# A transformer block kernel: the norm's power moved from before the first projection to behind it

## The chip, the cores and the metric

The kernel runs on one core of one Trainium2 chip. The metric is the device time of one execution in microseconds (us). A core has TensorE (PE, matrix products, reads SBUF and writes PSUM), VectorE (DVE), ScalarE (ACT), GpSimd (POOL) and the DMA queues that SyncE (SP) and ScalarE issue. Each engine works through a program of its own in order and waits on semaphores that others raise.

## The reference, cut to what matters

The computation is two transformer blocks on 512 tokens of width 1024. The first has a mixer (sparse attention with compressed keys, and a gated MLP) and a feed-forward layer; the second has differential attention, pooling, 32 experts and a gated embedding. The change touches only the first norm and the projection w_in (1024 to 2328 columns) behind it:

```
def rms_norm(x, g):
    y = xf * lax.rsqrt(jnp.mean(xf * xf, axis=-1, keepdims=True) + RMS_EPS)
    return (y * g.astype(jnp.float32)).astype(x.dtype)
...
    proj = jnp.einsum("bsd,de->bse", h, w_in)      # h = rms_norm(x, norm_mix_pre)
    q, k_c, v_c, k_s, v_s, k_w, v_w, gate_logits, u, v = jnp.split(proj, points, axis=-1)
...
    z_u = jax.nn.gelu(u)
    z_v = layer_norm(jax.nn.gelu(v), gmlp_ln_g, gmlp_ln_b)
```

The factor rsqrt(mean + eps) belongs to a token, the gain g to a column of x. So the factor may be put on the tokens ahead of the projection or on its outputs.

## The kernel before, in words

Everything runs as one program without loops at run time. Each weight matrix is streamed by SP as chunks of up to 128x2048 floats into three slots of RING (`sp_load`, L218). A chunk is split into a high part WH (ScalarE, `act_split`, L230) and a low remainder WL (VectorE, `dve_split`, L245), and each product is made of three matmuls (high by high, high by low, low by high: `pe_mm3`, L255 to L257). Chunk c+3 is loaded into the slot of chunk c once its low part is made.

Start (`*_start`): SP loads the tokens X as four tiles of 128 (L567). ScalarE issues the small loads (constants CST with the identity, nine rows of gains and tables, L570 to L579), then squares the four tiles with a running sum (L584). VectorE turns each sum into a mean (L655), POOL raises it to the power -0.5 (L598, into R4), and VectorE multiplies the tile by it (`rows`, L659, into XR0). TensorE transposes the 84 rows of gains (L603, from VectorE's copy L668 they are in GT) and then the four normed tiles, 8 transposes each, to the 8 banks PS0 to PS7 (L609). Bank j then holds rows 128j of the transposed tokens for all 512 tokens. ScalarE writes each bank times the gain as high part (`act_put`, L327), VectorE the low part (`dve_put`, L334).

Projection (`*_win`): the columns come in groups of two chunks (the upper and the lower half of the 1024 rows). Chunks 0 and 1 make 3 outputs of 128 columns by 512 tokens (compressed keys and values k_c and v_c, and k_s) in banks 0 to 2; chunks 2 and 3 make the 4 outputs of q in banks 0 to 3; chunks 4 and 5 make k_w in bank 3 and 4 outputs of 128 tokens by 280 columns in banks 4 to 7; chunks 6 to 9 are the first weights of the compression, used as they come (L749); chunks 10 to 13 make u and v. An output of a chunk with 512 free columns is 4 rows of weights by 3 matmuls, 12 in all. Behind single outputs `behind` lets TensorE make pieces of the position bias from a table: one "far" product (L620), four "near" groups of 64 small matmuls (L627) and four "cmp" groups of 31 (L634), all in bank 7, each copied by VectorE (L639, L643, L650) before the next may write the bank. The near groups stand behind outputs of chunks 1 and 2, the cmp groups behind outputs 2 and 3 of chunk 2 and outputs 0 and 1 of chunk 3.

The outputs of chunks 1, 3 and 5 leave PSUM by ScalarE (L780, L786, L799, L801). ScalarE issues DMAs of k_c and v_c to the other half of the partitions (L784). In `dve_win` VectorE makes, in this order: the far copy, the low part of chunk 3, the near and cmp copies, `blocks(0)` (4 additions of position rows to k_c, L861, waiting for those DMAs), the low part of chunk 4, `blocks(1)`, the low part of chunk 5. TensorE waits for the low part of a chunk before its first matmul.

## Time and profile before

| | |
|---|---|
| median of 3 runs | 2118.5 us (2116.66 to 2118.97) |
| the profiled execution's own time | 2118.25 us |
| its span | 2116.4 us |
| PE busy | 2060.8 us (97%) |
| DVE busy | 1537.0 us (73%) |
| ACT busy | 1383.2 us (65%) |
| chain that ended last | PE 91%, DVE 5%, issue 1%, ACT 1%, DMA 1% |

All times in the rows are microseconds from the span's start unless marked ns. Matmuls overlap, so one's duration is longer than its distance to the next.

### The profile page before, as it was taken

Reading aid. Unit: us, or ns where it says so; the run is one execution under the profiler, and the core shown is the slowest. Engines: PE = TensorE matmul, PEld = TensorE weight load, DVE = VectorE, ACT = ScalarE, POOL = GpSimd, SP = SyncE. Lnnn points to the kernel's source line nnn. Section 1 sums busy time; section 2 is a strip of 40 time slices with the busy share of each in tenths; the row PEclk is TensorE's granted clock in tenths of the full one; section 3 lists DMA queues with packets and bytes.
Section 4 is the critical chain, followed back from the end, with each engine's and each line's share of the span. In section 5 each row is a group of like instructions: output and inputs, shape, how many; then the busy total and the mean of one; then the engine's idle time right before and its main releaser. Section 6 shows DMA issues by size and latency. Waiting matters only on the chain.

```text
span 2116.4 us, 31589 instructions
## 1 busy us (share of the span) xinstructions
PE 2060.8 (97%) x10497; PEld 1707.9 (81%) x10497; DVE 1537.0 (73%) x1825; ACT 1383.2 (65%) x1870; POOL 194.8 (9%) x232
## 2 busy tenths in 40 slices
PE   7998899999999999899999999999999999999998
PEld 6887788888887887778888888888888888888877
DVE  4357743332325677789899999989898989898984
ACT  3247643222323447478888888888888888888863
POOL 0000000000000000111111111111111111111110
PEclk9999999999999999999999999999999999999999
DMA  6321013222323311489999999999999999999971
GB/s 199 135 71 61 21 55 124 87 94 80 120 100 103 117 72 41 171 307 373 369 372 367 370 369 371 369 366 375 366 379 363 370 372 372 361 371 371 376 264 40
DMA packets 86560, 511.27 MB, mean 242 GB/s; under 512 B 17285, under 2 KB 18905, under 8 KB 29146
## 3 DMA queue, kind: packets, MB, share of 16 engines
q1 hardware_dynamic: 71312, 487.61, 61.2%
q0 software_dynamic: 9680, 17.33, 3.2%
q10 hardware_dynamic: 5498, 5.39, 0.9%
q8 instruction: 45, 0.74, 0.1%
q14 instruction: 25, 0.20, 0.0%
HBM read 503.44 MB, written 23.07 MB: 249 GB/s over the span
## 4 chain that ended last, share of the span: by engine, by line
PE 91%; DVE 5%; issue 1%; ACT 1%; DMA 1%; ACTq 0%; POOL 0%; DVEq 0%; SPq 0%; POOLq 0%
PE PS L2595 17%; PE PS L2597 17%; PE PS L2596 17%; PE PS L255 10%; PE PS L257 10%; PE PS L256 10%; PE PS L2478 1%; PE PS L2592 1%; PE PS L2605 1%; PE PS L1153 1%; PE PS L1865 1%; DVE AR L1124 1%; PE PS L1082 0%; PE PS L1800 0%; PE PS L1793 0%
## 5 line engine op out<-in xcount | busy, mean ns | idle before, releaser
L2472 DVE TENSOR_TENSOR WL<-RING,WH 128x2048 fp32r<-128x2048 f32 x385 | 873.5, 2288 | 95.6 <-ACT WH L2452 92.5
L2452 ACT ACTIVATE WH<-RING 128x1024 fp32r<-128x1024 f32 x770 | 806.4, 1059 | 163.1 <-PE PS L2597 157.5
L2595 PE MATMUL PS<-WH,RA 128*128 128x512 f32 x1540 | 628.5, 408 | 0.0
L2597 PE MATMUL PS<-WH,RA 128*128 128x512 f32 x1540 | 600.7, 390 | 0.0
L2596 PE MATMUL PS<-WL,RA 128*128 128x512 f32 x1540 | 600.4, 390 | 0.0
L2597 PEld LDWEIGHTS PS<-WH,RA 128*128 128x128 f32 x1540 | 289.5, 188 | 61.7
L2596 PEld LDWEIGHTS PS<-WL,RA 128*128 128x128 f32 x1540 | 289.9, 188 | 58.1
L2595 PEld LDWEIGHTS PS<-WH,RA 128*128 128x128 f32 x1540 | 290.8, 189 | 55.3
L255 PE MATMUL PS<-WH,RA 128*128 128x512 f32 (+1 forms) x560 | 219.4, 392 | 3.4 <-DVE WL L245 2.2
L257 PE MATMUL PS<-WH,RA 128*128 128x512 f32 (+1 forms) x560 | 216.1, 386 | 0.0
L256 PE MATMUL PS<-WL,RA 128*128 128x512 f32 (+1 forms) x560 | 215.8, 385 | 0.0
L250 DVE SCALAR_TENSOR_TENSOR WL<-RING,GT,WH 128x512 fp32r<-128x512 f32 x120 | 82.2, 747 | 167.7 <-ACT WH L235 167.6
L235 ACT ACTIVATE WH<-RING,GT 128x512 fp32r<-128x512 f32 x120 | 76.8, 713 | 175.2 <-PE PS L257 175.2
L255 PE MATMUL PS<-RA,WH 128*128 128x512 f32 (+1 forms) x448 | 168.7, 377 | 3.3 <-DVE RA L458 1.6
L256 PE MATMUL PS<-RA,WH 128*128 128x512 f32 (+1 forms) x448 | 167.6, 374 | 0.0
L257 PE MATMUL PS<-RA,WL 128*128 128x512 f32 (+1 forms) x448 | 167.6, 374 | 0.0
L245 DVE TENSOR_TENSOR WL<-RING,WH 128x2048 fp32r<-128x2048 f32 (+3 forms) x29 | 62.3, 2150 | 92.0 <-ACT WH L230 91.8
L255 PEld LDWEIGHTS PS<-WH,RA 128*128 128x128 f32 x560 | 105.7, 189 | 24.1 <-DVE WL L245 2.3
L257 PEld LDWEIGHTS PS<-WH,RA 128*128 128x128 f32 x560 | 105.7, 189 | 21.2
L256 PEld LDWEIGHTS PS<-WL,RA 128*128 128x128 f32 x560 | 105.8, 189 | 20.2 <-issue 0.2
L230 ACT ACTIVATE WH<-RING 128x2048 fp32r<-128x2048 f32 (+3 forms) x29 | 52.1, 1801 | 105.5 <-PE PS L257 95.9
L2757 POOL DMA_INDIRECT acc_scr<-AR,SMALL x32 | 69.9, 2185 | 464.8 <-issue 464.8
(395 smaller groups left out, 2265.9 us busy)
## 6 DMA issues: line engine op xcount, KB each, us to landing
RING<-w_experts SPq DMA_DIRECT2D x390, 1024.0 KB, 7.3
RING<-w_front SPq DMA_DIRECT2D x58, 1024.0 KB, 4.9
X<-x SPq DMA_DIRECT2D x4, 512.0 KB, 5.6
...
```

The costliest lines, as they stand in the source:

```text
L235: x = e.activation(WH[:, ch.buf, v], RING[:, ch.slot, v], ACT.Copy, scale=GT[:, g:g + 1])
L245: x = e.tensor_tensor(WL[:, ch.buf, 0:n], RING[:, ch.slot, 0:n], WH[:, ch.buf, 0:n].bitcast(F32), ALU.subtract)
L250: x = e.scalar_tensor_tensor(WL[:, ch.buf, v], RING[:, ch.slot, v], GT[:, g:g + 1], WH[:, ch.buf, v].bitcast(F32), ALU.mult, ALU.subtract)
L255: e.matmul(out, a[0], b[0], start=start, stop=False)
L256: e.matmul(out, a[0], b[1], start=False, stop=False)
L257: return e.matmul(out, a[1], b[0], start=False, stop=stop)
L2452: e.activation(WH[:, m % 3, v], RING[:, m % 6, v], ACT.Copy).then_inc(s("m_hi"), 1)
L2472: e.tensor_tensor(WL[:, m % 3, :], RING[:, m % 6, :], WH[:, m % 3, :].bitcast(F32), ALU.subtract).then_inc(s("m_lo"), 1)
L2595: e.matmul(PS[bank][:, :], lhs[0][:, kr + k, :], WH[:, m % 3, c], start=(sel is None and kr == 0 and k == 0), stop=False)
L2596: e.matmul(PS[bank][:, :], lhs[0][:, kr + k, :], WL[:, m % 3, c], start=False, stop=False)
L2597: x = e.matmul(PS[bank][:, :], lhs[1][:, kr + k, :], WH[:, m % 3, c], start=False, stop=(stop and k == 3))
L2757: e.indirect_dma_start(acc_d, bass.IndirectOffsetOnAxis(TCOL, 0), YY, None, bounds_check=511, oob_is_err=False, compute_op=ALU.add).then_i ...
```

## The change: what it does

The transposes read the tokens X as they are loaded. Only the 8 rows of the first gain are waited for ahead of them; the 84 rows are transposed behind output 0 of chunk 0 (`pe_gains`), which waits until all 8 low parts of the tokens are made, because it writes bank 7. The squares, means and powers come behind that work on their engines. Chunk 0 is split in two halves, between the second and the third of the 8 tiles of tokens.

VectorE multiplies the identity by each token tile's power (RDG), TensorE multiplies an all-ones block by it (`pe_norm_row`, behind output 1 of chunk 1), and VectorE copies the result to RROW: every partition then holds the 512 powers. The eight outputs that have tokens as columns leave PSUM by VectorE, times RROW (`dve_project_out`), and no longer by ScalarE. The outputs that have tokens as rows take the power as a per-partition factor of the instruction that evicted them already (the copies of VSG, the activations of u and v).

The bias groups move: the far product to output 0 of chunk 2, the near groups to outputs 1 to 3 of chunk 2 and output 0 of chunk 3, the cmp groups 0 and 1 to outputs 1 and 2 of chunk 3, and both of the cmp groups 2 and 3 behind its output 3 (group 3 in bank 6).

```diff
-            e.wait_ge(s("w_lo"), ch.split + 1)
+            e.wait_ge(*((s("w_lo"), ch.split + 1) if c else (s("w_lo0"), 1)))
...
+                    if c == 0 and o == 0 and k == 2:
+                        e.wait_ge(s("w_lo"), 1)
...
-            for n, g in enumerate(("norm_mix_pre", "norm_ffn_pre", "attn_norm_2", "ffn_norm_2", "ple_gate_norm_2")):
-                e.dma_start(AR[n * 8:n * 8 + 8, 0:128], A[g].rearrange("o (a b) -> (o a) b", b=128)).then_inc(s("d_gr"), 16)
+            e.dma_start(AR[0:8, 0:128], A["norm_mix_pre"].rearrange("o (a b) -> (o a) b", b=128)).then_inc(s("d_g0"), 16)
+            for n, g in enumerate(("norm_ffn_pre", "attn_norm_2", "ffn_norm_2", "ple_gate_norm_2")):
+                e.dma_start(AR[n * 8 + 8:n * 8 + 16, 0:128], A[g].rearrange("o (a b) -> (o a) b", b=128)).then_inc(s("d_gr"), 16)
...
+            e.wait_ge(s("v_win"), AT["v_gt"] + 1)
+            for j in range(8):
+                if j == 2:
+                    e.wait_ge(s(f"w_ld{CH[0].slot}"), CH[0].loaded)
+                    for half in range(2):
+                        v = slice(CH[0].w * 2 * half, CH[0].w * (2 * half + 2))
+                        e.activation(WH[:, CH[0].buf, v], RING[:, CH[0].slot, v], ACT.Copy).then_inc(s(("w_hi0", "w_hi")[half]), 1)
+                act_put(e, XT["mix"] + j, j, PS[j][:, :], GT[:, j:j + 1])
+            act_split(e, 1)
             for i in range(4):
                 e.wait_ge(s(f"d_x{i}"), 16)
                 if i >= 2:
                     e.wait_ge(s("a_ss"), i - 1)
                 e.activation(WK[:, (i % 2) * 1024:(i % 2) * 1024 + 1024], X[:, i, :], ACT.Square,
                              accum_out=SSN[:, i:i + 1]).then_inc(s("a_ss"), 1)
-            act_split(e, 0)
-            e.wait_ge(s("v_win"), AT["v_gt"] + 1)
-            for j in range(8):
-                act_put(e, XT["mix"] + j, j, PS[j][:, :], GT[:, j:j + 1])
-            act_split(e, 1)
             act_split(e, 2)
+        RDG = cols(o_v, 4, 128)
+        RROW = VC.rearrange("p g h d -> p (g h d)")
+        def dve_project_out(e, n, dst):
+            bank = (0, 1, 2, 0, 1, 2, 3, 3)[n]
+            e.wait_ge(s("p_pr"), CH[(1, 1, 1, 3, 3, 3, 3, 5)[n]].first_out + (1, 2, 3, 1, 2, 3, 4, 1)[n])
+            if dst is None:
+                e.scalar_tensor_tensor(QT[:, bank, :], PS[bank][:, :], 0.125, RROW, ALU.mult, ALU.mult).then_inc(s("v_ev"), 1)
+            else:
+                e.tensor_tensor(dst, PS[bank][:, :], RROW, ALU.mult).then_inc(s("v_ev"), 1)
...
-            e.wait_ge(s("d_gr"), 16 * 9)
-            e.transpose(PS[7][:, 0:84], GR, IDT[0:84, 0:84]).then_inc(s("p_tab"), 1)
+            e.wait_ge(s("d_g0"), 16)
+            e.transpose(PS[7][:, 0:8], GR[0:8, :], IDT[0:8, 0:8]).then_inc(s("p_tab"), 1)
             for i in range(4):
-                e.wait_ge(s("v_xr"), i + 1)
+                e.wait_ge(s(f"d_x{i}"), 16)
                 for j in range(8):
                     if i == 0 and j == 7:
                         e.wait_ge(s("v_win"), AT["v_gt"] + 1)
-                    x = e.transpose(PS[j][:, i * 128:(i + 1) * 128], XR0[i][:, j * 128:(j + 1) * 128], IDT)
+                    x = e.transpose(PS[j][:, i * 128:(i + 1) * 128], X[:, i, j * 128:(j + 1) * 128], IDT)
                     if i == 3:
                         x.then_inc(s("p_xt"), 1)
+        def pe_gains(e):
+            e.wait_ge(s("d_gr"), 16 * 8)
+            e.wait_ge(s("v_xt"), XT["mix"] + 8)
+            e.transpose(PS[7][:, 0:84], GR, IDT[0:84, 0:84]).then_inc(s("p_tab"), 1)
+        def pe_norm_row(e):
+            for i in range(4):
+                e.wait_ge(s("v_dg"), i + 1)
+                x = e.matmul(PS[6][:, 128 * i:128 * i + 128], CST[:, 377:378].broadcast_to([128, 128]), RDG[:, i, :], start=True, stop=True)
+            x.then_inc(s("p_nr"), 1)
...
-            e.wait_ge(s("v_win"), AT["v_bf"] + 5 + i)
+            e.wait_ge(s("v_win"), AT["v_bf"] + 5 + min(i, 2))
             for c in range(31):
                 off = 511 + 128 * i - 16 * c - 31
-                x = e.matmul(PS[7][:, c * 8:c * 8 + 8], OH2[0:97, off:off + 128], T3[0:97, 24:32], start=True, stop=True)
+                x = e.matmul(PS[7 - i // 3][:, c * 8:c * 8 + 8], OH2[0:97, off:off + 128], T3[0:97, 24:32], start=True, stop=True)
...
-            def rows(i):
-                e.wait_ge(s("g_r4"), POW["mix"] + i)
-                e.tensor_scalar(XR0[i], X[:, i, :], R4[:, i:i + 1], None, ALU.mult).then_inc(s("v_xr"), 1)
-
-            mean(0)
-            mean(1)
-            rows(0)
-            mean(2)
-            rows(1)
-            mean(3)
             e.wait_ge(s("p_tab"), AT["p_gt"] + 1)
-            e.tensor_copy(GT[:, 0:84], PS[7][:, 0:84]).then_inc(s("v_win"), 1)
-            rows(2)
-            rows(3)
-            dve_split(e, 0)
+            e.tensor_copy(GT[:, 0:8], PS[7][:, 0:8]).then_inc(s("v_win"), 1)
             for j in range(8):
+                if j == 2:
+                    for half in range(2):
+                        v = slice(CH[0].w * 2 * half, CH[0].w * (2 * half + 2))
+                        e.wait_ge(s(("w_hi0", "w_hi")[half]), 1)
+                        e.tensor_tensor(WL[:, CH[0].buf, v], RING[:, CH[0].slot, v], WH[:, CH[0].buf, v].bitcast(F32), ALU.subtract
+                                        ).then_inc(s(("w_lo0", "w_lo")[half]), 1)
                 dve_put(e, XT["mix"] + j, j, PS[j][:, :], GT[:, j:j + 1])
             dve_split(e, 1)
+            for i in range(4):
+                mean(i)
+            for i in range(4):
+                e.wait_ge(s("g_r4"), POW["mix"] + i)
+                e.tensor_scalar(RDG[:, i, :], IDT, R4[:, i:i + 1], None, ALU.mult).then_inc(s("v_dg"), 1)
             dve_split(e, 2)
+            e.wait_ge(s("p_nr"), 1)
+            e.tensor_copy(RROW, PS[6][:, :]).then_inc(v_c.sem, v_c.up())
+            e.wait_ge(v_c.sem, v_c.n)
+            dve_project_out(e, 0, KCT[0])
+            e.wait_ge(s("p_tab"), AT["p_gt"] + 2)
+            e.tensor_copy(GT[:, 0:84], PS[7][:, 0:84]).then_inc(s("v_win"), 1)
...
+            def gains(e, o):
+                if o == 0:
+                    pe_gains(e)
+            pe_project(e, 0, outs, XP, 0, 8, {n: [("v_xt", XT["mix"] + n + 1)] for n in range(3)}, xt, behind=gains)
             def biases(e, o):
+                if o == 1:
+                    pe_norm_row(e)
+            def more_biases(e, o):
                 if o == 0:
                     pe_bias_far(e)
                 else:
                     pe_bias_near(e, o - 1)
-            def more_biases(e, o):
-                if o < 2:
-                    pe_bias_near(e, o + 2)
-                else:
-                    pe_bias_cmp(e, o - 2)
-
             pe_project(e, 1, outs, XP, 4, 8, {}, xt, behind=biases)
             outs = [(m, PS[m][:, :], "w", m * 128, 128) for m in range(4)]
-            free = {0: [("a_win", AT["a_kct"] + 1)], 1: [("a_win", AT["a_kct"] + 2)], 2: [("a_win", AT["a_kts"] + 1)]}
+            free = {0: [("v_ev", AT["v_kct"] + 1)], 1: [("v_ev", AT["v_kct"] + 2)], 2: [("v_ev", AT["v_kts"] + 1)]}
             def last_biases(e, o):
-                if o < 2:
-                    pe_bias_cmp(e, 2 + o)
+                if o == 0:
+                    pe_bias_near(e, 3)
+                else:
+                    pe_bias_cmp(e, o - 1)
+                if o == 3:
+                    pe_bias_cmp(e, 3)
             pe_project(e, 2, outs, XP, 0, 8, free, {}, behind=more_biases)
             pe_project(e, 3, outs, XP, 4, 8, {}, {}, behind=last_biases)
             outs = [(3, PS[3][:, :], "w", 0, 128)] + [(4 + i, PS[4 + i][:, 0:280], i, 128, 280) for i in range(4)]
-            free = {3: [("a_win", AT["a_q"] + 4)], 7: [("v_win", AT["v_bc"] + 4)]}
+            free = {3: [("v_ev", AT["v_q"] + 4)], 6: [("v_win", AT["v_bc"] + 4)], 7: [("v_win", AT["v_bc"] + 3)]}
...
-                e.activation(KCT[n], PS[n][:, :], ACT.Copy).then_inc(s("a_win"), 1)
-            e.activation(KT4[:, 0, :], PS[2][:, :], ACT.Copy).then_inc(s("a_win"), 1)
-                e.activation(QT[:, m, :], PS[m][:, :], ACT.Copy, scale=0.125).then_inc(s("a_win"), 1)
-            e.activation(KT4[:, 2, :], PS[3][:, :], ACT.Copy).then_inc(s("a_win"), 1)
...
+                e.activation(U[:, i, :], PS[4 + i][:, :], ACT.Gelu_apprx_tanh, scale=R4[:, i:i + 1]).then_inc(s("a_win"), 1)
+                e.activation(V[:, i, :], PS[4 + i][:, :], ACT.Gelu_apprx_tanh, scale=R4[:, i:i + 1], accum_out=LNS[:, i:i + 1]).then_inc(s("a_win"), 1)
...
+            dve_project_out(e, 1, KCT[1])
+            dve_project_out(e, 2, KT4[:, 0, :])
             dve_bias_far(e)
             dve_split(e, 3)
             for kb in range(4):
                 dve_bias_near(e, kb)
-            for i in range(4):
-                dve_bias_cmp(e, i)
+            dve_project_out(e, 3, None)
+            dve_bias_cmp(e, 0)
+            dve_project_out(e, 4, None)
+            dve_bias_cmp(e, 1)
+            dve_project_out(e, 5, None)
+            dve_bias_cmp(e, 2)
+            dve_project_out(e, 6, None)
+            dve_bias_cmp(e, 3)
             blocks(0)
             dve_split(e, 4)
             blocks(1)
             dve_split(e, 5)
+            dve_project_out(e, 7, KT4[:, 2, :])
             for i in range(4):
                 e.wait_ge(s("p_pr"), CH[5].first_out + 2 + i)
-                e.tensor_copy(VSG[:, i, :], PS[4 + i][:, 0:280]).then_inc(s("v_win"), 1)
+                e.tensor_scalar(VSG[:, i, :], PS[4 + i][:, 0:280], R4[:, i:i + 1], None, ALU.mult).then_inc(s("v_win"), 1)
             for n in range(2):
                 e.memset(HID[n][:, :, :, 31:32], 0.0).then_inc(v_c.sem, v_c.up())
+            e.wait_ge(s("v_ev"), AT["v_kw"] + 1)
```

## Rows read from the trace of the kernel before

**Rows 1.** The page: busy time and share by engine, and the chain that ended last.
```profile
PE 2060.8 (97%) x10497; PEld 1707.9 (81%) x10497; DVE 1537.0 (73%) x1825; ACT 1383.2 (65%) x1870; POOL 194.8 (9%) x232
...
PE 91%; DVE 5%; issue 1%; ACT 1%; DMA 1%; ACTq 0%; POOL 0%; DVEq 0%; SPq 0%; POOLq 0%
```

**Rows 2.** The timeline of PE, 10 to 19: start, busy, line, count, [idle before].
```profile
10.14 0.37 PE L603 MATMUL PS<-CST,AR 84*128 84x84 f32 x1 [10.14 <-DMA AR<-gmlp_b_s]
11.15 6.22 PE L609 MATMUL PS<-CST,AR 128*128 128x128 f32 x32 [0.63 <-DVE AR L659]
18.31 0.47 PE L255 MATMUL PS<-RA,WH 128*128 128x512 f32 x1 [0.95 <-DVE RA L334]
```

**Rows 3.** Line L609 in two stretches, 14.2 to 14.7 and 16.6 to 17.0 (ns).
```profile
L609 PE MATMUL PS<-CST,AR x5: 421/421/421, 13.8 to 14.7; 128*128 128x128 f32 x5
...
L609 PE MATMUL PS<-CST,AR x6: 272/272/273, 16.4 to 17.0; 128*128 128x128 f32 x6
```

**Rows 4.** The timeline of DMA issues at the start, on ScalarE's and SP's queues.
```profile
1.17 0.57 ACTq L572 DMA_DIRECT2D AR<-norm_mix_pre  x1
...
4.71 0.40 ACTq L576 DMA_DIRECT2D AR<-gmlp_b_s  x1
```

**Rows 5.** Issue to landing: CST (L570), the tokens (L567), chunk 0 (L218, issued 2.99).
```profile
DMA to landing us min/median/max: 4.3/4.3/4.3
...
DMA to landing us min/median/max: 4.2/5.6/7.2
...
DMA to landing us min/median/max: 8.1/8.1/8.1
```

**Rows 6.** The timeline of ScalarE at the start.
```profile
8.05 1.06 ACT L584 ACTIVATE AR<-X 128x1024 f32<-128x1024 f32 x1
...
12.23 1.47 ACT L230 ACTIVATE WH<-RING 128x1536 fp32r<-128x1536 f32 x1
16.70 4.74 ACT L327 ACTIVATE RA<-PS,GT 128x512 fp32r<-128x512 f32 x8 [3.00 <-PE PS L609]
```

**Rows 7.** The timeline of VectorE at the start.
```profile
14.06 1.75 DVE L245 TENSOR_TENSOR WL<-RING,WH 128x1536 fp32r<-128x1536 f32 x1
17.42 5.36 DVE L334 SCALAR_TENSOR_TENSOR RA<-PS,GT,RA 128x512 fp32r<-128x512 f32 x8 [1.60 <-ACT RA L327]
22.84 4.09 DVE L245 TENSOR_TENSOR WL<-RING,WH 128x1536 fp32r<-128x1536 f32 x2
```

**Rows 8.** The timeline of PE, 60 to 70: the end of chunk 3, the start of chunk 4.
```profile
60.80 0.93 PE L634 MATMUL PS<-AR 97*128 97x8 bf16 x31
61.59 0.48 PE L255 MATMUL PS<-RA,WH 128*128 128x512 f32 x1
...
66.68 0.39 PE L256 MATMUL PS<-RA,WH 128*128 128x512 f32 x1
66.91 0.39 PE L257 MATMUL PS<-RA,WL 128*128 128x512 f32 x1
68.08 0.47 PE L255 MATMUL PS<-RA,WH 128*128 128x512 f32 x1 [0.78 <-ACT AR L799]
```

**Rows 9.** The timeline of VectorE and of ScalarE's queue around the cmp copies.
```profile
30.16 2.88 ACTq L784 DMA_DIRECT2D AR<-AR  x4
...
58.16 0.41 DVE L650 COPY AR<-PS 128x248 f32<-128x248 f32 x1 [3.20 <-PE PS L634]
...
62.11 3.90 DVE L861 TENSOR_TENSOR AR<-AR,GT 64x496 f32<-64x496 f32 x4
66.04 1.86 DVE L245 TENSOR_TENSOR WL<-RING,WH 128x1632 fp32r<-128x1632 f32 x1
```

**Rows 10.** The timeline of PE at the gap ahead of chunk 10.
```profile
102.64 0.80 PE L255 MATMUL PS<-WH,RA 128*128 128x512 f32 x1 [2.18 <-DVE WL L245]
```

**Rows 11.** Busy time in stretches: PE, PEld, DVE, ACT, POOL, granted clock, DMA share, GB/s.
```profile
107.00:108.00 1.00, 1.00 (x4) 0.74 (x3) 0.00 (x0) 0.98 (x2) 0.00 (x0) 0.50 0.83 172
108.00:109.00 1.00, 1.00 (x10) 1.00 (x8) 0.22 (x1) 0.89 (x1) 0.00 (x0) 0.80 0.78 279
```

More of the change, by code:

```diff
@@ L184, in program @@
         for parts in (
-                (("p_gt", 1), ("p_bf", 5), ("p_bc", 4)),
+                (("p_gt", 2), ("p_bf", 5), ("p_bc", 4)),
                 (("p_kc", 1), ("p_vc", 1), ("p_gm", 8)),
-                (("a_kct", 2), ("a_kts", 1), ("a_q", 4), ("a_kw", 1), ("a_hid", 2), ("a_sg", 1), ("a_u", 4), ("a_v", 4), ("a_lnv", 4)),
+                (("a_hid", 2), ("a_sg", 1), ("a_u", 4), ("a_v", 4), ("a_lnv", 4)),
+                (("v_kct", 2), ("v_kts", 1), ("v_q", 4), ("v_kw", 1)),
                 (("a_lam", 1), ("a_rope", 2), ("a_sr", 1), ("a_gk", 1)),
@@ L196, in program @@
                 (("v_lam", 2), ("v_ang", 1), ("v_sr", 1)),
-                (("v_gt", 1), ("v_t3", 1), ("v_bf", 5), ("v_bc", 4), ("v_blk", 8), ("v_vw", 4), ("v_hidr", 1), ("v_kc", 1), ("v_vc", 1), ("v_lnm", 1), ("v_wst", 2), ("v_zv", 1), ("v_gm", 8)),
+                (("v_gt", 2), ("v_t3", 1), ("v_bf", 5), ("v_bc", 4), ("v_blk", 8), ("v_vw", 4), ("v_hidr", 1), ("v_kc", 1), ("v_vc", 1), ("v_lnm", 1), ("v_wst", 2), ("v_zv", 1), ("v_gm", 8)),
         ):
@@ L554, in program @@
         KORD = [(x, p) for x in (0, 2, 1, 3) for p in range(2)]
-        XR0 = [ar(o_qt + 1024 * i, 1024) for i in range(4)]
         RS = ATS[:, 80:144]
@@ L649, in dve_bias_cmp @@
             e.wait_ge(s("p_tab"), AT["p_bc"] + i + 1)
-            e.tensor_copy(BC[:, i, :, 0:31], PS[7][:, 0:248].rearrange("p (c h) -> p h c", h=8)).then_inc(s("v_win"), 1)
+            e.tensor_copy(BC[:, i, :, 0:31], PS[7 - i // 3][:, 0:248].rearrange("p (c h) -> p h c", h=8)).then_inc(s("v_win"), 1)
         def dve_start(e):
@@ L710, in pe_win @@
             outs = [(n, PS[n][:, :], "w", n * 128, 128) for n in range(3)]
-            pe_project(e, 0, outs, XP, 0, 8, {n: [("v_xt", XT["mix"] + n + 1)] for n in range(3)}, xt)
+            def gains(e, o):
+                if o == 0:
+                    pe_gains(e)
+            pe_project(e, 0, outs, XP, 0, 8, {n: [("v_xt", XT["mix"] + n + 1)] for n in range(3)}, xt, behind=gains)
             def biases(e, o):
+                if o == 1:
+                    pe_norm_row(e)
+            def more_biases(e, o):
                 if o == 0:
@@ L745, in pe_win @@
                         if c % 2 == 0:
-                            e.wait_ge(*((s("a_win"), AT["a_q"] + 1 + 2 * n + m), (s("a_win"), AT["a_kw"] + 1))[n * m])
+                            e.wait_ge(*((s("v_ev"), AT["v_q"] + 1 + 2 * n + m), (s("v_ev"), AT["v_kw"] + 1))[n * m])
                         for k in range(8):
@@ L778, in act_win @@
             for n in range(2):
-                e.wait_ge(s("p_pr"), CH[1].first_out + n + 1)
-                e.activation(KCT[n], PS[n][:, :], ACT.Copy).then_inc(s("a_win"), 1)
-                e.wait_ge(s("a_win"), AT["a_kct"] + n + 1)
+                e.wait_ge(s("v_ev"), AT["v_kct"] + n + 1)
                 for g in range(2):
@@ L784, in act_win @@
                         e.dma_start(KK[n][64 * par:64 * par + 64, g, :], KCT[n][64 * g:64 * g + 64, :]).then_inc(s(f"d_kk{n}"), 16)
-            e.wait_ge(s("p_pr"), CH[1].first_out + 3)
-            e.activation(KT4[:, 0, :], PS[2][:, :], ACT.Copy).then_inc(s("a_win"), 1)
-            e.wait_ge(s("a_win"), AT["a_kts"] + 1)
+            e.wait_ge(s("v_ev"), AT["v_kts"] + 1)
             for half in range(2):
@@ L796, in act_win @@
             act_split(e, 5)
-            for m in range(4):
-                e.wait_ge(s("p_pr"), CH[3].first_out + m + 1)
-                e.activation(QT[:, m, :], PS[m][:, :], ACT.Copy, scale=0.125).then_inc(s("a_win"), 1)
-            e.wait_ge(s("p_pr"), CH[5].first_out + 1)
-            e.activation(KT4[:, 2, :], PS[3][:, :], ACT.Copy).then_inc(s("a_win"), 1)
-            e.wait_ge(s("a_win"), AT["a_kw"] + 1)
+            e.wait_ge(s("v_ev"), AT["v_kw"] + 1)
             for half in range(2):
@@ L873, in dve_win @@
             dve_split(e, 5)
+            dve_project_out(e, 7, KT4[:, 2, :])
             for i in range(4):
                 e.wait_ge(s("p_pr"), CH[5].first_out + 2 + i)
-                e.tensor_copy(VSG[:, i, :], PS[4 + i][:, 0:280]).then_inc(s("v_win"), 1)
+                e.tensor_scalar(VSG[:, i, :], PS[4 + i][:, 0:280], R4[:, i:i + 1], None, ALU.mult).then_inc(s("v_win"), 1)
             for n in range(2):
                 e.memset(HID[n][:, :, :, 31:32], 0.0).then_inc(v_c.sem, v_c.up())
+            e.wait_ge(s("v_ev"), AT["v_kw"] + 1)
             e.memset(VC, 0.0).then_inc(v_c.sem, v_c.up())
@@ L936, in pe_cmp_logits @@
                 e.wait_ge(s("v_win"), AT["v_kc"] + 1)
-                e.wait_ge(s("a_win"), AT["a_q"] + 4)
+                e.wait_ge(s("v_ev"), AT["v_q"] + 4)
             for par in range(2):
```

2 lines of the change are left out of this document (removed).

## The prediction

> **What bounds the kernel now.** I read the page first: TensorE is busy for 97% of the span and makes 91% of the chain that ended last [rows 1]. So a microsecond by which TensorE's work starts later or earlier near the beginning moves the end by about as much, as long as nothing behind it has slack to give back. The change touches the first 110 us only, so I then read, in this order, the timeline of each engine over the first 70 us and the chain of waits there, the DMA landings, and the granted clock by stretches. The reader is to see three places. First, the transposes begin at 11.15, the first projection matmul at 18.31, and TensorE runs from there without a gap worth the name until chunk 4 [rows 2, 8]. Second, at chunk 4 TensorE stands 0.78 us for ScalarE's eviction of q, and the low part of chunk 4 comes from VectorE at just the same time (66.04 + 1.86 = 67.9, against a start at 68.08) [rows 8, 9]. Third, a gap of 2.18 us at 102.6 is followed by 5.7 us in which the granted clock is 0.50 of full [rows 10, 11].
>
> **The start.** The transposes no longer wait for squares, powers and the normed copy; they wait for the constants (issued 0.72, landed 4.3 later: 5.0), the first token tile (0.71 + 4.2 = 4.9) and the first gain row. That row's landing is in no row; it is issued at 1.17 [rows 4, 5]. Between the constants' 4.3 us and the 5.4 us of the last gain row (issued 4.71, waited for until 10.14 [rows 2, 4]) it lands at 5.5 to 6.6; I take 5.6, nearer its neighbour in the queue. The last token tile lands at about 2.1 + 7.2 = 9.3 [rows 5]. One transpose takes the engine about 0.22 us (five start between 13.8 and 14.7) and later 0.11 (six between 16.4 and 17.0) [rows 3]: the column of the granted clock reads 1.00 before its first recorded change, but the durations of 421 and then 272 ns say that the first 5 us of TensorE's work went at the lower level, 1.2 GHz. ScalarE can write its first tile after the 25th transpose: 5.6 + 0.3 for the gain row + 25 x 0.216 = 11.3, somewhat less if the clock rises on the way. I take 10.9 (bounds 10.3 and 12.2). Before it was 16.70 [rows 6], so 5.8 us are won here.
>
> **What is given back at once.** The split of chunk 0, formerly done during the transposes (12.23 to 15.8 [rows 6, 7]), now stands between tile 2 and tile 3. Chunk 0 has landed (2.99 + 8.1 = 11.1 [rows 5]). The halves cost VectorE 1.75 / 2 = 0.9 each, ScalarE 0.75 each. VectorE is the slower of the two with 5.36 / 8 = 0.67 a tile [rows 7]: its first low tile starts 0.72 after ScalarE's first, the first half's low part is ready at 10.9 + 0.72 + 1.34 + 0.9 = 13.9, and the eighth tile at 10.9 + 0.72 + 5.4 + 1.8 = 18.8. TensorE starts at 14.0, runs rows 0 and 1, gets tile 3 at 15.6 and ends output 0 at 15.6 + 6 x 0.227 = 17.0 (0.227 is the distance of two matmuls at the full clock [rows 8]). There the moved transpose of the 84 gain rows waits for the eighth low tile, because it writes bank 7: 1.8 us of idle TensorE, with outputs 1 and 2 queued behind it. With 0.37 for the transpose [rows 2] and 24 x 0.227, chunk 0 ends at 24.6. Before it ended at 18.31 + 36 x 0.227 = 26.5. Of 5.8 us, 1.9 are left.
>
> **Squares, means, powers, identity times power, RROW.** ScalarE's four squares (1.06 each [rows 6]) now follow the split of chunk 1 and end near 23; TensorE asks for the result behind output 1 of chunk 1, at about 30, so POOL's powers and the four small products on VectorE have some 7 us of cover and I cost them at nothing. `pe_norm_row` is new on TensorE: 4 matmuls of the transposes' size, 0.11 to 0.22 each [rows 3], and the change of operand around them: 0.7 us (bounds 0.4 and 1.2). The copy to RROW and the first eviction on VectorE (2 x 0.7, as the puts of 128x512 from PSUM [rows 7]) are ready 1.4 us after it; TensorE has output 2 (2.7 us) meanwhile. The second and third evictions stand behind the table's small conversions, still ahead of chunk 2's second output. The eight evictions cost VectorE the same 0.6 to 0.75 each that they cost ScalarE, and there is idle VectorE time between the near copies. The factors in VSG, u and v ride in instructions that exist already: nothing (bounds 0 and 0.1 us each). The x, constant and RING loads keep their order and their queues.
>
> **Chunk 4, where the loss is.** Before, the last cmp copy was over at about 62.1, and `blocks(0)` (3.90) and the low part of chunk 4 (1.86) were hidden behind outputs 2 and 3 of chunk 3 [rows 9]. Now cmp groups 2 and 3 are issued by TensorE only behind output 3, and VectorE's program has the copies of both, and the eviction of output 3, ahead of `blocks(0)`. Call t the end of output 3, before at 67.14. After, t = 67.14 - 1.9 (won) + 0.7 (norm row) - 2 x 0.79 (two cmp groups that now come behind t; 0.79 is 61.59 - 60.80 [rows 8]) = 64.4. From t on: cmp group 2 on TensorE 0.95, its copy 0.4, the eviction 0.75, the copy of group 3 0.4 [rows 9], `blocks(0)` 3.9, the low part 1.9. Chunk 4 starts at t + 8.3 = 72.7, against 68.08 before: 4.6 us later, with TensorE idle for about 6.6 us. Chunk 5's low part follows 5.8 us later and has chunk 4's 8.9 us of matmuls as cover. Everything behind (the gap at 102.6 as well, which hangs on chunk 7's end, a load and a split) is released by TensorE's own progress, so it moves with it.
>
> **The clock.** After the 2.18 us gap the granted clock stood at 0.50, that is 1.2 GHz, from about 102 to 108.4 [rows 10, 11]; TensorE worked 5.7 us in it and did half of that: 2.85 us lost. A gap three times as long should cost it again: I add 2.8 (bounds 0, if the clock holds, and 2.9). In the start there are two more gaps, 2.5 us between transposes and first matmul and 1.8 us behind output 0; before it was 0.95 [rows 2]. Whether the clock is low in chunk 0's last two outputs I can't read off; I add 1.0 (bounds 0 and 2.9).
> The Trainium skill speaks against the change here: its page "TensorE: Matmul & The Clock Gate", section "HAM oscillation — how this bites in real kernels", says that an idle wait between bursts of matmuls puts TensorE back to half rate, and that the burst behind it starts cold each time. By that rule the 2.8 us are due, without it the sum is 2123.7; the trace agrees, with its 0.50 behind a gap of 2.18 us.
>
> **The sum.** 4.6 + 2.8 + 1.0 = +8.4 us on the profiled execution's own 2118.25 (span 2116.4 and 1.85 around it), which lies 0.25 below the median of the three: about 2126.6 us.
>
> **The rivals.**
> *The clock holds over the gap.* Chunk 4 starts 4.6 later and little else: 2118.25 + 4.6 + (0 to 1.0) = 2123 to 2124. For it: a gap of 0.95 us left no trace in the clock. Against: 2.18 us did. Chance 0.14.
> *Low clock at both ends.* The start's gaps cost their full 2.9, and a shifted later gap one more such stretch: 2128.5 to 2131. Chance 0.12.
> *VectorE gets past the late copies, so the change is faster.* Place: `blocks(0)` and the low part of chunk 4 (5.8 us of VectorE). If they ran before cmp group 2, TensorE would stand only for the eviction, t + 2.1 at 66.5, and the end would be 1.6 earlier: 2116.6. It decides in favour as soon as VectorE has started them by t - 4. For it: their inputs, the DMAs issued at 30.16, are there long before. Against: in the trace VectorE sat 3.20 us ahead of a cmp copy with the same inputs already there, so it does not reorder [rows 9]. Chance 0.07.
> The Trainium skill says the same in "TensorE: Matmul & The Clock Gate", section "Architectural detail: the array is 16× 32×32, not 1× 128×128": ScalarE and VectorE are strict first in, first out; by it this rival would have no chance.
> *The start wins more than I give it.* If the gain transposes found the eighth low tile ready (VectorE's tiles and halves overlapping better) and the clock were high from early on, up to 4 us of the 5.8 stay and the sum is 2118.25 + 4.6 - 2.1 + (0 to 2.8) = 2120.7 to 2123.5, and about 2118.5 with a shorter wait at chunk 4. Chance 0.10.
> My forecast has 0.57.
>
> **How the numbers follow.** A measurement of this kernel can't tell less than 0.2%, 4.2 us, from no change. Slower by more: the forecast, the low clock, most of the held clock and a third of the last: 0.81. Within: 0.12. Faster by more: only the passing VectorE with a larger start gain: 0.07. The range 2121.0 to 2130.0 leaves out the faster cases and the tail of the two slow stretches.
>
> **What would show it.** After: the first transpose near 5.6, ScalarE's first tile near 10.9, the first projection matmul near 14, a gap of about 2 us in front of the transposed gains, chunk 0 ending near 24.6; then an idle TensorE of 6 to 7 us in front of chunk 4 with VectorE's low part as releaser, and a granted clock of 0.50 in the first microseconds of chunk 4. I am wrong if that gap is below 2 us, if the clock reads 1.00 behind it, or if the start is won by more than 4 us.

## The result, and the profile after

The changed kernel is slower. Its median is 2128.78 us (7 runs, 2124.7 to 2134.15), that of the kernel before in the same rounds 2120.73 (7 runs, 2116.66 to 2125.32); the ratio is 1.0041 with a 95% interval of 1.0026 to 1.0056. The forecast was +8.4 us, 2126.6 (2121.0 to 2130.0); the medians differ by 8.05.

The profiled execution of the changed kernel took 2130.72 us, 12.5 more than the one before, so it is one of its longer ones. Its page, busy time by engine and the chain that ended last, answers to [rows 1]:

```profile
PE 2069.6 (97%) x10506; PEld 1715.0 (81%) x10506; DVE 1541.0 (72%) x1836; ACT 1378.3 (65%) x1863; POOL 195.0 (9%) x232
...
PE 91%; DVE 5%; DMA 2%; issue 1%; ACT 1%; POOL 0%; SPq 0%; ACTq 0%; DVEq 0%; POOLq 0%
```

The timeline of TensorE at the start (start, busy, line, count, [idle before]) answers to [rows 2]; L629 is now the transpose, L257 to L259 the three matmuls of a product:

```profile
5.43 0.24 PE L623 MATMUL PS<-CST,AR 8*128 8x8 f32 x1 [5.43 <-DMA AR<-norm_mix_pre]
5.60 5.59 PE L629 MATMUL PS<-CST,X 128*128 128x128 f32 x32
14.86 0.50 PE L257 MATMUL PS<-RA,WH 128*128 128x512 f32 x1 [3.67 <-DVE WL L697]
...
16.98 0.63 PE L258 MATMUL PS<-RA,WH 128*128 128x512 f32 x1
17.40 0.63 PE L259 MATMUL PS<-RA,WL 128*128 128x512 f32 x1
...
19.77 0.26 PE L640 MATMUL PS<-CST,AR 84*128 84x84 f32 x1 [0.46 <-DVE RA L338]
19.83 0.48 PE L257 MATMUL PS<-RA,WH 128*128 128x512 f32 x1
```

The transposes begin 5.5 us earlier, the first projection matmul 3.45 us earlier, output 1 of chunk 0 at 19.83. The reader is to see two things: 3.67 us of idle TensorE between them, and matmuls 0.42 apart from 16.98 on, the distance of the lower clock. ScalarE's timeline of the same stretch, against [rows 6], shows what stands in between:

```profile
10.51 1.28 ACT L331 ACT_TABLE_LOAD   x1 [10.51 <-PE PS L629]
11.81 1.27 ACT L331 ACTIVATE RA<-PS,GT 128x512 fp32r<-128x512 f32 x2
12.96 1.57 ACT L590 ACTIVATE WH<-RING 128x768 fp32r<-128x768 f32 x2
14.43 3.58 ACT L331 ACTIVATE RA<-PS,GT 128x512 fp32r<-128x512 f32 x6
```

The load of the activation table now comes behind the transposes and ahead of the first tile. Before, it was over ahead of the first square, while TensorE had nothing to do yet:

```profile
6.76 1.28 ACT L584 ACT_TABLE_LOAD   x1 [6.76 <-issue]
```

VectorE's timeline, against [rows 7], has the two halves of chunk 0 between its second and third tile:

```profile
12.53 1.41 DVE L338 SCALAR_TENSOR_TENSOR RA<-PS,GT,RA 128x512 fp32r<-128x512 f32 x2 [6.65 <-ACT RA L331]
13.85 1.82 DVE L697 TENSOR_TENSOR WL<-RING,WH 128x768 fp32r<-128x768 f32 x2
15.59 4.04 DVE L338 SCALAR_TENSOR_TENSOR RA<-PS,GT,RA 128x512 fp32r<-128x512 f32 x6
```

TensorE's timeline around the start of chunk 4, against [rows 8]:

```profile
64.80 0.39 PE L259 MATMUL PS<-RA,WL 128*128 128x512 f32 x1
65.03 1.71 PE L667 MATMUL PS<-AR 97*128 97x8 bf16 x62
72.97 0.80 PE L257 MATMUL PS<-RA,WH 128*128 128x512 f32 x1 [6.23 <-DVE WL L247]
```

And VectorE's timeline at the same place, against [rows 9] (L683 cmp copy, L609 eviction of q, L895 `blocks`, L247 low part):

```profile
66.00 0.42 DVE L683 COPY AR<-PS 128x248 f32<-128x248 f32 x1 [2.60 <-PE PS L667]
66.33 0.68 DVE L609 SCALAR_TENSOR_TENSOR AR<-PS,AR 128x512 f32<-128x512 f32 x1
66.93 0.41 DVE L683 COPY AR<-PS 128x248 f32<-128x248 f32 x1
67.25 3.77 DVE L895 TENSOR_TENSOR AR<-AR,GT 64x496 f32<-64x496 f32 x4
71.06 1.86 DVE L247 TENSOR_TENSOR WL<-RING,WH 128x1632 fp32r<-128x1632 f32 x1
```

VectorE stands idle for 2.60 us ahead of the cmp copy, and then has 6.9 us of work that TensorE waits for. The busy time by stretches (PE, PEld, DVE, ACT, POOL, granted clock, DMA share, GB/s), against [rows 11]:

```profile
66.00:68.00 2.00, 0.74 (x30) 0.64 (x26) 2.00 (x4) 0.00 (x0) 0.00 (x0) 0.88 0.00 0
68.00:70.00 2.00, 0.00 (x0) 0.00 (x0) 1.97 (x3) 0.00 (x0) 0.00 (x0) 0.50 0.00 0
...
74.00:76.00 2.00, 2.00 (x6) 1.61 (x5) 1.97 (x3) 0.00 (x0) 0.00 (x0) 0.50 0.79 266
...
78.00:80.00 2.00, 2.00 (x17) 1.96 (x16) 0.58 (x1) 0.00 (x0) 0.00 (x0) 1.00 0.28 45
```

The clock falls inside the gap and is back after TensorE has worked for nearly 5 us. I compare kernels from here on at marks along TensorE's program. Of the first raw product of chunk 6 (L749 before, L792 after) and the first product with the band matrix of the second block (L1554, L1598) these are the rows by line (durations in ns, then first and last start); first the kernel before, then the changed one:

```profile
L749 PE MATMUL PS<-AR,RING x128: 215/275/275, 86.1 to 100.2; 128*128 128x62 f32 x128
...
L1554 PE MATMUL PS<-RING,AR x32: 270/275/275, 753.1 to 769.8; 128*128 128x128 f32 x32
...
L2595 PE MATMUL PS<-WH,RA x1540: 387/389/632, 901.9 to 2044.1; 128*128 128x512 f32 x193
```

```profile
L792 PE MATMUL PS<-AR,RING x128: 215/275/275, 93.2 to 107.3; 128*128 128x62 f32 x128
...
L1598 PE MATMUL PS<-RING,AR x32: 270/275/275, 759.7 to 776.5; 128*128 128x128 f32 x32
...
L2639 PE MATMUL PS<-WH,RA x1540: 389/389/984, 913.4 to 2057.4; 128*128 128x512 f32 x193
```

The shift is 4.9 us at chunk 4 (68.08 to 72.97), 7.2 at chunk 6 (86.06 to 93.22), 6.7 at the band product, and 11.5 at the first expert product (the last line of each fence). Nothing was changed between the last two marks: there the kernel routes tokens. The two profiled executions differ in it by 5 us, and whether that belongs to the change was the open question of the experiments.

### The profile page after: what moved, and what is told of

It is laid out like the page before. It is cut to its first block, busy times and chain, and to the rows that moved or that the text cites. A ratio compares the mean times of both kernels' runs of the same rounds, so it can differ in the third digit from the quotient of the medians.

```text
span 2128.9 us, 31614 instructions
## 1 busy us (share of the span) xinstructions
PE 2069.6 (97%) x10506; PEld 1715.0 (81%) x10506; DVE 1541.0 (72%) x1836; ACT 1378.3 (65%) x1863; POOL 195.0 (9%) x232
## 4 chain that ended last, share of the span: by engine, by line
PE 91%; DVE 5%; DMA 2%; issue 1%; ACT 1%; POOL 0%; SPq 0%; ACTq 0%; DVEq 0%; POOLq 0%
PE PS L2639 17%; PE PS L2641 16%; PE PS L2640 16%; PE PS L257 10%; PE PS L259 10%; PE PS L258 10%; PE PS L2522 1%; PE PS L2636 1%; PE PS L2649 1%; PE PS L1197 1%; PE PS L1909 1%; DVE AR L1168 1%; PE PS L1126 1%; PE PS L1844 1%; DMA AR<-ffn_norm 0%
## 5 line engine op out<-in xcount | busy, mean ns | idle before, releaser
L257 PE MATMUL PS<-WH,RA 128*128 128x512 f32 (+1 forms) x560 | 219.4, 392 | 3.1 <-DVE WL L247 1.9
L259 PE MATMUL PS<-WH,RA 128*128 128x512 f32 (+1 forms) x560 | 216.1, 386 | 0.0
L257 PE MATMUL PS<-RA,WH 128*128 128x512 f32 (+1 forms) x448 | 170.4, 380 | 11.5 <-DVE WL L247 6.2
L259 PE MATMUL PS<-RA,WL 128*128 128x512 f32 (+1 forms) x448 | 168.8, 377 | 0.0
L247 DVE TENSOR_TENSOR WL<-RING,WH 128x2048 fp32r<-128x2048 f32 (+3 forms) x28 | 60.6, 2164 | 92.5 <-ACT WH L232 92.4
L257 PEld LDWEIGHTS PS<-WH,RA 128*128 128x128 f32 x560 | 105.7, 189 | 23.9 <-DVE WL L247 2.0
L259 PEld LDWEIGHTS PS<-WH,RA 128*128 128x128 f32 x560 | 105.7, 189 | 21.1
```

Of the source, the lines that this page charges most:

```text
L247: x = e.tensor_tensor(WL[:, ch.buf, 0:n], RING[:, ch.slot, 0:n], WH[:, ch.buf, 0:n].bitcast(F32), ALU.subtract)
L257: e.matmul(out, a[0], b[0], start=start, stop=False)
L259: return e.matmul(out, a[1], b[0], start=False, stop=stop)
```

## The experiments

Theory A: the loss is VectorE's order at chunk 4 plus the low clock behind the gap; the start wins some and the two add up along TensorE's chain. Theory B: the loss comes from the stage near 860 to 930. All comparisons stand in one table behind the experiments.

**e1: only the late cmp groups, in the kernel before.**

```diff
             def more_biases(e, o):
                 if o < 2:
                     pe_bias_near(e, o + 2)
-                else:
-                    pe_bias_cmp(e, o - 2)
...
             def last_biases(e, o):
-                if o < 2:
-                    pe_bias_cmp(e, 2 + o)
+                if o >= 1:
+                    pe_bias_cmp(e, o - 1)
+                if o == 3:
+                    pe_bias_cmp(e, 3)
```

> The kernel before with one thing of the change: the four cmp groups of the position bias come behind outputs 1, 2 and 3 (two) of chunk 3. Theory A (VectorE's order costs: with the last cmp copies late, blocks(0) and the low part of chunk 4 lose their cover): chunk 4 starts at 65.6 + 8.5 = 74.1 instead of 68.1, the clock falls to 0.50 behind the gap, and the first product with the band matrix in the second block (753.1 before, 759.7 in the changed kernel) stands at about 761.5, the time is 8 to 9 us above before. Theory B (the loss is in the routing stage near 870 to 930, where the changed kernel's profile shows another 6 us, or in the moved norm itself): that product stays within 1 us of 753, the time within 2 us of before.

The timeline of TensorE in e1 at chunk 4:

```profile
66.49 0.93 PE L634 MATMUL PS<-AR 97*128 97x8 bf16 x31 [0.51 <-DVE AR L650]
73.51 0.80 PE L255 MATMUL PS<-RA,WH 128*128 128x512 f32 x1 [6.08 <-DVE WL L245]
```

The placement alone makes a gap of 6.08 us, moves chunk 4 by 5.4 us and the band product by 9.3 (753.1 to 762.4), and the time has a ratio of 1.0036 (1.0024 to 1.0048). That is theory A; theory B allowed 2 us. It also shows that this one edit costs as much as the whole change, as far as the two intervals can tell.

**e2: the changed kernel with VectorE's order mended.** Two halves of `blocks(0)` stand in the idle times ahead of the cmp copies, and the low part of chunk 4 in the next; `blocks` counts on a semaphore of its own.

```diff
...
             dve_project_out(e, 3, None)
+            blocks(0, (0,))
             dve_bias_cmp(e, 0)
             dve_project_out(e, 4, None)
+            blocks(0, (1,))
             dve_bias_cmp(e, 1)
             dve_project_out(e, 5, None)
-            dve_bias_cmp(e, 2)
+            dve_split(e, 4)
             dve_project_out(e, 6, None)
+            dve_bias_cmp(e, 2)
             dve_bias_cmp(e, 3)
-            blocks(0)
-            dve_split(e, 4)
             blocks(1)
```

> The changed kernel with VectorE's order mended: the additions of blocks(0) stand behind the evictions of outputs 0 and 1 of chunk 3, the low part of chunk 4 behind that of output 2, and the last eviction before the two last cmp copies. Theory A: chunk 4 starts at about 66.8 (before 68.1, changed 73.0), right behind the last cmp group, without a fall of the clock there; the band product stands at 751 to 752, the time is 1 to 2 us below before and 8 below the changed kernel. Theory B: chunk 4 starts early too, but the time stays 5 us or more above before.

TensorE's timeline in e2, then the same stretch on VectorE:

```profile
66.40 1.71 PE L667 MATMUL PS<-AR 97*128 97x8 bf16 x62
67.96 0.48 PE L257 MATMUL PS<-RA,WH 128*128 128x512 f32 x1
```

```profile
61.18 1.93 DVE L895 TENSOR_TENSOR AR<-AR,GT 64x496 f32<-64x496 f32 x2
...
64.81 1.85 DVE L247 TENSOR_TENSOR WL<-RING,WH 128x1632 fp32r<-128x1632 f32 x1
66.59 0.69 DVE L609 SCALAR_TENSOR_TENSOR AR<-PS,AR 128x512 f32<-128x512 f32 x1
```

The gap is gone and chunk 4 follows the last cmp group. In this execution the first projection matmul started 0.6 us later (15.48 against 14.86) and the low clock lay over all of output 0 of chunk 0; output 3 of chunk 3 ended 1.4 us later than in the changed kernel's profile (66.40 against 65.03), and chunk 4 came at 67.96, not 66.8. The band product stands 1.5 us ahead of before, as expected. The time is 2119.08 us against 2119.64 for the kernel before, ratio 0.9994 (0.9985 to 1.0004): about 10 us less than the changed kernel's ratio of 1.0041 gives, and no gain over before that the runs can tell.

**e3: the gap filled.** 26 matmuls whose result nobody reads go behind the last cmp group.

```diff
                 if o == 3:
                     pe_bias_cmp(e, 3)
+                    for _ in range(26):
+                        e.matmul(PS[4][:, :], WH[:, CH[3].buf, 0:128], XP[0][:, 0, :], start=True, stop=True)
```

> The changed kernel with 26 more matmuls of 128x512 (results unused) behind the last cmp group, 5.9 us of work in the gap. What the clock alone costs: chunk 4 starts at 73.0 as in the changed kernel, but at a granted clock of 1.00, and the raw products of chunk 6 begin 2.3 us earlier than its 93.2, at 90.9; the band product at 757.5. If the clock has no part, they stay at 93.2 and 759.7.

TensorE's timeline in e3 and the busy time of a stretch of it:

```profile
67.73 6.15 PE L776 MATMUL PS<-RA,WH 128*128 128x512 f32 x26
74.23 0.50 PE L257 MATMUL PS<-RA,WH 128*128 128x512 f32 x1 [0.35 <-DVE WL L247]
```

```profile
74.00:76.00 2.00, 1.77 (x8) 1.46 (x9) 2.00 (x3) 0.00 (x0) 0.00 (x0) 1.00 0.40 66
```

Chunk 4 comes even later than in the changed kernel (74.23, again after a low clock in chunk 0), and chunk 6 starts earlier, at 92.27. From chunk 4 to chunk 6 it takes 18.0 us at the full clock, the same as before (86.06 - 68.08 = 18.0), and 20.25 in the changed kernel (93.22 - 72.97). So the low clock behind the gap costs 2.2 to 2.3 us. The time fell too: ratio 1.0022 (1.0013 to 1.0032), against 1.0041 for the changed kernel; whether it fell by more than those 2.3 us, the overlapping intervals can't tell.

**e4: the activation table loaded early.**

```diff
+            e.wait_ge(s("d_c"), 16)
+            e.activation(GT[:, 87:88], CST[:, 0:1], ACT.Copy)
             e.wait_ge(s("v_win"), AT["v_gt"] + 1)
```

> The changed kernel with one small activation of a column of the constants ahead of ScalarE's first tile, so that the activation table's load (1.28 us, at 10.51 to 11.79 in the changed kernel, in the chain) comes while TensorE transposes. Theory A of the start (each piece of the chain transposes, table, tiles and halves on VectorE counts in full): ScalarE's first tile at 10.5 instead of 11.8, first projection matmul at 13.6 instead of 14.9, chunk 4 at 71.7 and the band product at 758.4, 1.3 us earlier, the time 1.3 lower. Rival: the wait of the gain transposes or the low clock takes it back and chunk 4 starts at 73.0 again.

ScalarE's timeline in e4, then TensorE's:

```profile
6.97 1.28 ACT L585 ACT_TABLE_LOAD   x1 [6.97 <-issue]
8.26 0.20 ACT L585 ACTIVATE GT<-CST 128x1 f32<-128x1 f32 x1
10.87 1.26 ACT L331 ACTIVATE RA<-PS,GT 128x512 fp32r<-128x512 f32 x2 [2.41 <-PE PS L631]
```

```profile
13.92 0.80 PE L257 MATMUL PS<-RA,WH 128*128 128x512 f32 x1 [2.38 <-DVE WL L699]
...
72.05 0.79 PE L257 MATMUL PS<-RA,WH 128*128 128x512 f32 x1 [6.23 <-DVE WL L247]
```

The first tile comes 0.94 earlier and so does chunk 4 (0.92): the piece counts in full down the chain; it is less than 1.28 because the transposes ended 0.36 later in this execution. The time by medians (2126.84, ratio 1.0034, 1.002 to 1.0048) can't be told from the changed kernel's.

**e5, e6, e7: the changed kernel again, both mends, and the gain transpose moved.** e6 is e2 and e4 together; e7 has besides

```diff
             def gains(e, o):
-                if o == 0:
+                if o == 2:
                     pe_gains(e)
```

> The changed kernel once more, on the chip of the two mended ones. Theory A: chunk 4 behind a gap of 6 to 7 us at 73 (0.7 either way with the clock in chunk 0), the band product (753.1 before) at 759 to 760.5, the time 7 to 8 us above before. If the routing stage was the cause, the band product may stand there but the end of the experts must be 12 us late again, as in the first profile; by theory A only 6.7 us late or with a scatter of both signs around it.

> The changed kernel with VectorE's order mended (as e2) and the activation table loaded early (as e4). Theory A: the two gains add up, since they lie one behind the other in TensorE's chain: chunk 4 at 66.4 to 67 (before 68.1, e2 68.0), the band product at 750 to 751, the time 2 to 3 us below before. Rival: the low clock in chunk 0 takes the table's 1.3 us back and the product stands at 751.6 as in e2.

> As e6, and the transpose of the 84 gain rows behind output 2 of chunk 0, so that it no longer waits for the eighth low tile. Theory A: that wait was 0.4 to 0.5 us in the changed kernel and nothing where the clock was low in chunk 0, so between 0 and 0.5 us: the band product at 750 to 750.5, the time within 0.5 us of e6.

e5 repeats the loss: chunk 4 at 73.6, band product 7.7 us late, ratio 1.0054 (1.0041 to 1.0067), and its profiled execution, the fastest of its five, reaches the first expert product 7.7 us late too, not 11.5. So theory B falls as the cause of the loss: the extra of the first profile is not in every execution. e6 and e7 have the front better than expected: chunk 6 3.1 and 2.4 us ahead of before, the band product of e6 4.4 us ahead. But their times are those of before, where 2 to 3 us less was expected: 1.0003 (0.9994 to 1.0012) and 0.9998 (0.9987 to 1.0009). In e7 the profiled execution lost its lead by the band product (753.7, expected at 750) between 250 and 680, where the clock was at 0.50 three more times.

In e6 part of the lead went behind the band product (4.4 us there, 1.7 at the first expert product). The chain of waits of e6, and below it that of the changed kernel, has the load of the broadcast row ffn_norm in it (start, us, what), which the chain before has not:

```profile
855.39 7.68 DMA AR<-ffn_norm
...
863.67 1.99 PE PS L2158 x16
```

```profile
866.45 8.31 DMA AR<-ffn_norm
...
875.35 2.58 PE PS L2155 x16
```

It takes 6.6 us from issue to landing before, 7.5 in e2 and 6.2 in e5. What goes beyond 6.6 shows one for one: from the band product to the first router product it is 113.8 us before, 0.9 more in e2, 1.1 more in e6, 1.8 more in the changed kernel's first profile, and 0.1 less in e5. So the row explains 1.1 us of the 2.7 that e6 lost there and 1.8 of the 4.9 of the first profile; the next experiments ask for the rest.

**e8, e9, e10: the row's load moved ahead.** e10 is e7 once more. e8 is e7, e9 the kernel before, each with

```diff
-            for n, c in ((1, 61), (2, 62), (0, 63)):
+            for n, c in ((1, 61), (2, 62)):
                 e.wait_ge(s("w_lo"), CH[c].split + 1)
                 sp_expert_load(e, n, n, 0)
...
             e.dma_start(GROW, A["ffn_norm_2"].broadcast_to([128, 1024])).then_inc(s("d_rt"), 16)
+            e.wait_ge(s("w_lo"), CH[63].split + 1)
+            sp_expert_load(e, 0, 0, 0)
             sp_expert_load(e, 4, 4, 0)
```

> The mended kernel e7 with one more edit far behind the change: the loads of the router's weights and of the broadcast row ffn_norm go ahead of the wait for the low part of chunk 63, and so ahead of the expert load that shares the DMA engines with them. The question is where the 2.5 to 4.4 us go that e2, e6 and e7 have won at the band product and lost by the first expert product. Theory C (the row's landing, 6.6 us in before but 7.5 to 8.3 in e2, e6 and the first run of the changed kernel, ends last in the router stage, and the gap brings the low clock): the router product follows the end of the chain before it without a gap, the distance from the band product to the first expert product falls from 148.8 (before) and 151.4 (e2, e6) to 146 or less, the time is 4 us or more below before. Theory D (chance of the clock alone): the distance stays between 148 and 152 and the time within 1 us of e10.

> The control: the kernel before with the same moved loads. Theory C: the distance from band product to first expert product falls below 148.8 by what the router product waits there (0.7 to 2 us, and the low clock with it), time 1 to 3 us below before; the difference between e8 and e9 is then what the change itself is worth once mended, 3 to 4.5 us. Theory D: both unchanged.

> e7 once more, beside e8 and e9. Theory A for the front: the raw products of chunk 6 begin at 83 to 84 (before 86.1), the band product at 749 to 751 unless the clock falls once more on the way (e7: at 680). The time 0 to 2 us below before; the distance band product to first expert product 148 to 152.

The row's load in e8 by line, issued at 852.7, and its time to landing:

```profile
L2114 SPq DMA_DIRECT2D AR<-ffn_norm x1: 432/432/432, 852.7 to 852.7; - x1
...
DMA to landing us min/median/max: 4.6/4.6/4.6
```

e8 is the fastest kernel of the study: 2115.38 us against 2119.41 in the same rounds, ratio 0.9976 (0.9966 to 0.9987). e9 is as before, 0.9996 (0.9984 to 1.0007), where 1 to 3 us less was expected, and e10 as e7, 0.9998 (0.9985 to 1.0011). Measured against the kernel before, neither the mended change (e7, e10) nor the moved row (e9) is worth a measurable amount alone, and together they are worth 0.24%, 4 to 5 us.

The traces do not bear out theory C as the reason. The wait for the row is gone, and the router product comes 113.7 us behind the band product in e8, 114.3 in e10: that is 0.5 us. But the distance from the band product to the first expert product, forecast at 146 or less, is 150.5 us in e8's profiled execution and 150.1 in e9's, against 148.8 before and 150.8 in e10. Behind the router product e8 took 36.8 us and e10 36.5; before it was 35.0. Theory D had the distance right and missed the time, which it put within 1 us of e10's; it is 3.4 us below. What the distance does follow is the low clock. The busy time from 880 to 890, as in [rows 11], first before, then in e10 and in e8:

```profile
880.00:890.00 10.00, 7.41 (x65) 6.19 (x64) 7.53 (x26) 4.07 (x6) 1.46 (x1) 1.00 0.27 107
...
880.00:890.00 10.00, 4.35 (x39) 3.53 (x38) 8.27 (x31) 4.58 (x7) 2.90 (x3) 0.63 0.32 121
...
880.00:890.00 10.00, 5.13 (x52) 3.98 (x51) 6.93 (x26) 4.58 (x7) 1.46 (x1) 0.84 0.26 106
```

Added up over stretches of 1 us, the distance holds 10.2 us at a clock of 0.50 before and in e1, e3, e4 and e5 (148.8 to 149.1 us long), 13.7 to 15.4 in e9, e7 and e8 (149.2 to 150.5), 17.7 to 17.9 in e2, e6 and e10 (150.8 to 151.5), and 19.9 in the changed kernel's first profile (153.7).

The times of all executions point the same way. Within one kernel, a mean granted clock lower by 0.001 goes with a time longer by about 1.7 us: of the 29 executions of the kernel before beside e8, the four at 0.995 took 2116.9 us on average, the one at 0.990 took 2125.8. The means over executions are 0.9933 before, 0.9907 in e10, 0.9905 in e7 and 0.9927 in e8. Brought to 0.993 by that slope, which is an estimate, e8 stands at 2114.9, e10 at 2115.1, e9 and the kernel before at 2120.3. So by this estimate the mended change is worth 5 us with the row moved or not, and e7 and e10 lose it again to a lower clock. That e8's executions had the higher clock is on record; why, and whether moving the row brought it or chance did, no trace here shows.

| kernel | chunk 4 starts | chunk 6 | band product | first expert product | row to landing | mean clock | median us (runs) | ratio, 95% |
|---|---|---|---|---|---|---|---|---|
| before | 68.1 | 86.1 | 753.1 | 901.9 | 6.6 | 0.9933 | 2119.4 to 2120.7 | 1 |
| changed | 73.0 | 93.2 | 759.7 | 913.4 | 8.3 | 0.9886 | 2128.8 (7) | 1.0041 (1.0026, 1.0056) |
| e5, changed again | 73.6 | 93.9 | 760.8 | 909.6 | 6.2 | 0.9884 | 2130.9 (5) | 1.0054 (1.0041, 1.0067) |
| e1, late cmp alone | 73.5 | 94.4 | 762.4 | 911.2 | 7.1 | 0.9908 | 2127.3 (6) | 1.0036 (1.0024, 1.0048) |
| e2, order mended | 68.0 | 86.0 | 751.6 | 903.0 | 7.5 | 0.9920 | 2119.1 (12) | 0.9994 (0.9985, 1.0004) |
| e3, gap filled | 74.2 | 92.3 | 757.9 | 907.0 | 7.0 | 0.9922 | 2123.8 (11) | 1.0022 (1.0013, 1.0032) |
| e4, table early | 72.1 | 91.6 | 757.4 | 906.3 | 6.5 | 0.9895 | 2126.8 (8) | 1.0034 (1.002, 1.0048) |
| e6, e2 and e4 | 64.9 | 82.9 | 748.7 | 900.2 | 7.7 | 0.9912 | 2120.4 (11) | 1.0003 (0.9994, 1.0012) |
| e7, and gains later | 65.6 | 83.6 | 753.7 | 902.9 | 6.6 | 0.9905 | 2119.4 (12) | 0.9998 (0.9987, 1.0009) |
| e10, e7 again | 63.1 | 81.2 | 746.4 | 897.2 | 7.1 | 0.9907 | 2118.8 (12) | 0.9998 (0.9985, 1.0011) |
| e8, e7 and row early | 65.0 | 83.0 | 748.9 | 899.4 | 4.6 | 0.9927 | 2115.4 (12) | 0.9976 (0.9966, 0.9987) |
| e9, before and row early | 68.1 | 86.1 | 752.9 | 903.0 | 5.3 | 0.9936 | 2118.9 (12) | 0.9996 (0.9984, 1.0007) |

The marks and the row's landing are of one profiled execution each. The mean clock is the granted clock averaged over all executions of a kernel (before: the 29 beside e8; 0.9930 and 0.9933 in the other experiments). It counts low clock in idle time too, which costs nothing, so the slope above is not used for kernels with a gap at chunk 4.

## Why the prediction was right, and where its terms were off

*The sign, the place and the mechanism.* A wait of 6 to 7 us in front of chunk 4 with VectorE's low part as releaser was forecast at 72.7; it is 6.23 us and ends at 72.97. e1 shows that it comes from the cmp groups' place, e2 that VectorE's order is what makes it cost. That the end comes within 0.3 us is in part luck: output 3 of chunk 3 ended at 65.03, not 64.4, and from there it took 7.9 us, not 8.3.

*The start's first term.* The transposes began at 5.60 as taken, and the 25th ended at 10.5 (10.9 forecast). Then the working missed the table load: it had hidden between the DMA issues and the first square before, and the step "ScalarE can write its first tile after the 25th transpose" left it out. It costs 1.28 us in the chain (e4 took it out and won 0.9 down to chunk 4).

*The wait of the gain transpose* was forecast at 1.8 us with output 0 ending at 17.0; it is 0.46. Not because the eighth tile came early (it ended at 19.6 against 18.8), but because output 0 itself began 0.9 later and, its second half at the lower clock, ended at about 19.3. The two errors cancel in part: outputs 1 and 2 ended at 25.4 instead of 24.6, and the start won 1.2 us against 26.6, not 1.9. The low clock of chunk 0, carried as a term of 1.0 of its own, was mostly spent inside that wait. In e5 the whole of output 0 went at it, and there was no wait; chunk 4 came 0.7 us later than in the first profile (73.64 against 72.97), and 0.3 of that was there already at the first projection matmul (15.17 against 14.86). The forecast added wait and low clock one to the other where they overlap.

*The norm row* was 0.81 us of TensorE (30.80 to 31.61) against 0.7; the trace has 8 matmuls for the 4 in the kernel's code.

*The clock behind the gap* was forecast at 2.8 and measured at 2.2 to 2.3 by e3, because it returned after 4.8 us of work and not 5.7.

*The sum.* At chunk 6 the change costs 7.2 us in one execution and 7.8 in the other, at the band product 6.7 and 7.7, against 8.4. The medians say 8.05 in the first rounds and 11.5 in those of e5, so that the first came so near 8.4 is in part luck. The 1 to 4 us above the front's cost are not located. In the first profile 4.9 us came in the routing stage, with 19.9 us at the low clock there against 10.2 before; in e5's profile nothing came there. The stage's length varied between 148.8 and 153.7 us among the twelve profiled executions. A lower clock is the likely place: the mean is 0.9886 and 0.9884 against 0.9933, of which the 10.2 us at 0.50 around chunk 4 make 0.0024. Why the clock is lower elsewhere stays open. (The sum "without it" in the prediction, 2123.7, should be 2123.85; nothing hangs on it.)

*The rivals.* The clock did not hold. VectorE did not pass a waiting copy: it stood 2.60 us ahead of one with `blocks(0)` behind it. The start won less, not more. The low clock was there at both ends, as the second rival has it, but its cost at the start overlapped with the wait.
